# Silu in place on ScalarE, and the modulation pieces through ScalarE's DMA queue into three buffers

## What is computed

```
def swiglu(h, w_gate_up, w_down):
    gu = h @ w_gate_up
    gate, up = jnp.split(gu, 2, axis=-1)
    return (jax.nn.silu(gate) * up) @ w_down
```

```
mod = (jax.nn.silu(c.astype(F32)) @ ada_w.astype(F32) + ada_b.astype(F32)).astype(x.dtype)
```

## Time and profile before

| | |
|---|---|
| median of the timed runs | 1428.95 us |
| the profiled execution: own time, span | 1436.26 us, 1434.6 us |
| TensorE matmul busy | 1321.5 us (92%) |
| VectorE busy | 751.1 us (52%) |
| ScalarE busy | 510.2 us (36%) |
| GpSimd busy | 198.0 us (14%) |
| DMA | 364.40 MB, mean 254 GB/s |
| granted TensorE clock, mean | 0.968 of full speed |

### The profile page before, as it was taken

The page is one execution under the profiler, slowest core; times in us unless marked ns, Lnnn a source line. Parts: engine busy times, 40 slices in busy tenths (PEclk is TensorE's granted clock), DMA queues, the critical chain, the costliest instruction groups (busy, mean ns, idle before and its releaser), DMA issues.

```text
span 1434.6 us, 24642 instructions
## 1 busy us (share of the span) xinstructions
PE 1321.5 (92%) x10257; PEld 1017.1 (71%) x10260; DVE 751.1 (52%) x1297; ACT 510.2 (36%) x828; POOL 198.0 (14%) x96
## 2 busy tenths in 40 slices
PE   4989899799999799979998689999999999999997
PEld 3989899789899799878997579754444444444432
DVE  5767687657588768778994645511221212212113
ACT  2423333356543233347553542322222222222212
POOL 0000000000000000076866265100000000000002
PEclk7999999899999999989999999999999999999999
DMA  9776567243377806632422413619999999999994
GB/s 355 274 284 238 209 249 273 78 105 131 148 280 265 301 16 226 223 145 45 176 89 98 169 55 142 255 65 421 427 427 423 426 423 428 423 425 428 423 425 168
DMA packets 50640, 364.40 MB, mean 254 GB/s; under 512 B 7411, under 2 KB 8563, under 8 KB 23924
## 3 DMA queue, kind: packets, MB, share of 16 engines
q1 hardware_dynamic: 49828, 360.61, 63.3%
q0 software_dynamic: 720, 2.46, 0.9%
HBM read 360.35 MB, written 2.70 MB: 253 GB/s over the span
## 4 chain that ended last, share of the span: by engine, by line
PE 67%; DMA 12%; DVE 11%; issue 4%; ACT 3%; POOL 2%; SPq 0%; DVEq 0%; POOLq 0%
PE banks L1266 15%; DMA scr<-ada 9%; PE banks L724 9%; PE banks L726 8%; PE banks L725 8%; PE banks L1291 8%; PE banks L1217 4%; PE banks L1226 4%; DMA c_row<-small 2%; POOL slot_lo L636 2%; PE banks L702 1%; DVE scr L1764 1%; DVE slot_lo L1736 1%; PE banks L713 1%; PE banks L1232 1%
## 5 line engine op out<-in xcount | busy, mean ns | idle before, releaser
L726 PE MATMUL banks<-h_hi,slot_lo 128*128 128x256 f32 x704 | 200.3, 285 | 4.2 <-issue 4.2
L724 PE MATMUL banks<-h_hi,gu_hi 128*128 128x256 f32 x704 | 200.7, 285 | 3.2 <-issue 3.2
L725 PE MATMUL banks<-h_lo,gu_hi 128*128 128x256 f32 x704 | 200.2, 284 | 0.0
L2294 DVE TENSOR_TENSOR out_lo<-banks,out_hi 128x512 fp32r<-128x512 f32 x62 | 42.9, 692 | 185.2 <-ACT out_hi L1678 185.2
L726 PEld LDWEIGHTS banks<-h_hi,slot_lo 128*128 128x128 f32 x704 | 136.2, 193 | 4.5 <-issue 4.5
L724 PEld LDWEIGHTS banks<-h_hi,gu_hi 128*128 128x128 f32 x704 | 136.2, 193 | 4.0 <-issue 3.4
L726 PE MATMUL banks<-slot_lo,slot_lo 128*128 128x256 f32 x480 | 137.0, 285 | 0.0
L725 PEld LDWEIGHTS banks<-h_lo,gu_hi 128*128 128x128 f32 x704 | 136.2, 194 | 0.0
L724 PE MATMUL banks<-act_hi,down_hi 128*128 128x256 f32 x352 | 103.4, 294 | 20.6 <-DVE slot_lo L1736 20.6
L1291 PE MATMUL banks<-ring,scr 128*64 128x512 f32 x512 | 116.9, 598 | 1.9 <-ACT scr L1672 1.9
L1266 PE MATMUL banks<-ring,scr 128*64 128x512 f32 x512 | 112.6, 592 | 0.0
(11 more groups left out here) (418 smaller groups left out, 3001.1 us busy)
## 6 DMA issues: line engine op xcount, KB each, us to landing
ring<-experts SPq DMA_DIRECT2D x64, 2048.0 KB, 11.4
ring<-ws SPq DMA_DIRECT2D x77, 1536.0 KB, 7.1
ring<-experts SPq DMA_DIRECT2D x64, 1024.0 KB, 11.0
scr<-ada SPq DMA_DIRECT2D x96, 256.0 KB, 4.0
ring<-experts SPq DMA_DIRECT2D x1, 3072.0 KB, 9.9
scr<-bias_line POOLq DMA_DIRECT2D x4, 512.0 KB, 8.3
bias_line<-scr SPq DMA_DIRECT2D x1, 1536.0 KB
x<-xT SPq DMA_DIRECT2D x1, 1024.0 KB, 4.9
```

The lines of the kernel that those rows point to most:

```text
L724: nc.tensor.matmul(out, hi, move_hi, start=start, stop=False, skip_group_check=True)
L725: nc.tensor.matmul(out, hi, move_lo, start=False, stop=False, skip_group_check=True)
L726: return nc.tensor.matmul(out, lo, move_hi, start=False, stop=stop, skip_group_check=True)
L2294: ins = nc.vector.tensor_tensor(out_lo[part], B[6 + half], out_hi[part].bitcast(F32), ALU.subtract)
```

## The change

ScalarE makes `Silu` of the gate in place, so that VectorE's product L1781 and the tile `sig_f` in the network go. The 96 pieces and the four loads of `c_part` move from SyncE's queue to ScalarE's, with no wait of their own: ScalarE issues the pieces of step s+1 right behind the Silu of step s, ahead of the copy of the down weights. There are three buffers. VectorE takes all pieces of a step in one place, behind the split of gate and up: two or three in each of the steps 2 to 10. The sigmoid of `c` moves ahead of the first network, VectorE's product of it likewise, and `c_row` is written from ScalarE's queue behind `ffn_start`; ScalarE waits for it to land before it enters the network's loop. TensorE's part is unchanged.

```
-        c_part, ada_part = view(2304, ADA_COLS), [view(2816 + ADA_COLS * q, ADA_COLS) for q in range(2)]
+        c_part, ada_part = view(2304, ADA_COLS), [view(at, ADA_COLS) for at in (2816, 3328, 4352)]
...
+        ADA_STEPS = {s: range(8 * (s - 2) // 3, 8 * (s - 1) // 3) for s in range(2, RING)}
+        C_LOADS = 0
...
@@ SyncE: ada_before, ffn_2_ada and their calls go, and
-            sp.wait_ge(csil_ready, 1)
-            with nc.allow_non_contiguous_dma(reason="one column a chunk"):
-                sp.dma_start(c_row.rearrange("a (c p) -> p (a c)", p=P), csil).then_inc(csil_ready, 16)
-            sp.wait_ge(csil_ready, 17)
...
@@ ScalarE
                 if k in (1, 3, 6):
-                    load_table(ACT.Sigmoid)
+                    load_table(ACT.Silu if k < 6 else ACT.Sigmoid)
...
                         act.wait_ge(gr_ready, RING * i + (done + s + 1))
-                        nc.scalar.activation(sig_f[:, s % 2, :], gated[:, s % 2, :], ACT.Sigmoid).then_inc(sig_ready, 1)
+                        nc.scalar.activation(gated[:, s % 2, :], gated[:, s % 2, :], ACT.Silu).then_inc(sig_ready, 1)
+                        if s == 0:
+                            act.dma_start(c_part, c_row[0:1, bass.ds(ADA_COLS * i, ADA_COLS)].partition_broadcast(P)).then_inc(ada_landed[C_LOADS], 16)
+                        for p in ADA_STEPS.get(s + 1, ()):
+                            part = ada[ADA_PARTS * i + (2 * ADA_PARTS * (base // S_FFN2) + p)]
+                            act.dma_start(ada_part[p % 3], part).then_inc(ada_landed[p % 3], 16)
                         first_part(down_hi[s % 2], s, 2 * TILE, SLOT, down_hi_ready)
...
             norm_squares(0)
+            act.wait_ge(vec_loaded, 16)
+            nc.scalar.activation(csig, vecs[:, VEC["c"][0]:VEC["c"][1]], ACT.Sigmoid).then_inc(csil_ready, 1)
 
             act.wait_ge(pool_d, 4)
             ffn_start(S_FFN1)
+            act.wait_ge(csil_ready, 2)
+            with nc.allow_non_contiguous_dma(reason="one column a chunk"):
+                act.dma_start(c_row.rearrange("a (c p) -> p (a c)", p=P), csil).then_inc(csil_ready, 16)
             norm_squares(1, "norm_ffn0")
-            act.wait_ge(vec_loaded, 16)
-            nc.scalar.activation(csig, vecs[:, VEC["c"][0]:VEC["c"][1]], ACT.Sigmoid).then_inc(csig_ready, 1)
+            act.wait_ge(csil_ready, 18)
             ffn(S_FFN1, 0)
...
@@ VectorE
-                        modulation(s, 0, i)
+                        for p in ADA_STEPS.get(s, ()):
+                            modulation(p, i)
...
-                        step(1, nc.vector.tensor_tensor(gated[:, a, :], gated[:, a, :], sig_f[:, a, :], ALU.mult))
-                        step(2, nc.vector.tensor_tensor(act_raw, gated[:, a, :], up_r, ALU.mult))
-                        step(3, nc.vector.tensor_copy(act_hi[a], act_raw))
+                        dve.wait_ge(dve_step, 3 * RING * i + (steps[0] + 3 * s + 1))
+                        step(1, nc.vector.tensor_tensor(act_raw, gated[:, a, :], up_r, ALU.mult))
+                        step(2, nc.vector.tensor_copy(act_hi[a], act_raw))
                         nc.vector.tensor_tensor(act_lo[a], act_raw, act_hi[a].bitcast(F32), ALU.subtract).then_inc(act_ready, 1)
-                        modulation(s, 1, i)
                         dve.wait_ge(down_hi_ready, RING * i + (done + s + 1))
                         second_part(down_hi[a], s, 2 * TILE, SLOT, down_lo_ready)
-                        modulation(s, 2, i)
```

More of the change, by code:

```diff
@@ L356, in build @@
             sem(s) for s in ("s_ready", "s_used", "max_ready", "exp_ready", "p_ready", "pt_ready", "pts_ready", "o_ready", "o_copied"))
-        csig_ready, csil_ready, ada_used, mod_ready = (sem(s) for s in ("csig_ready", "csil_ready", "ada_weights_used", "mod_ready"))
-        ada_landed = [sem(f"ada_landed{q}") for q in range(2)]
+        csil_ready, ada_used, mod_ready = (sem(s) for s in ("csil_ready", "ada_weights_used", "mod_ready"))
+        ada_landed = [sem(f"ada_landed{q}") for q in range(3)]
         out_ready, out_done, rows_loaded, shared_done = (sem(s) for s in ("out_ready", "out_done", "rows_loaded", "shared_done"))
@@ L554, in _ @@
             load_after(S_FFN2 + 6, s_ready, HEADS_1 // 2)
-            def ffn_2_ada(units):
-                for unit in units:
-                    body, s = divmod(unit, RING)
-                    ada_before(s,
-                               lambda: sp.dma_start(c_part, c_row[0:1, body * ADA_COLS:(body + 1) * ADA_COLS].partition_broadcast(P)).then_inc(ada_landed[0], 16),
-                               lambda p: sp.dma_start(ada_part[p % 2], ada[ADA_PARTS * (2 + body) + p]).then_inc(ada_landed[p % 2], 16),
-                               lambda p: sp.wait_ge(ada_used, ADA_PARTS * (2 + body) + p + 2))
-            ada_units = 0
             for n in range(S_FFN2 + 7, N_SLOTS):
@@ L573, in _ @@
                         sp.dma_start(gate_row.rearrange("a (c p) -> p (a c)", p=P), mod[:, 40:48]).then_inc(rows_loaded, 16)
-                after = TENANT[n] + 1 if n >= S_FFN2 + RING else S_FFN2
-                if n < S_BR and after > S_FFN2 + ada_units:
-                    ffn_2_ada(range(ada_units, min(after - S_FFN2, FFN_CHUNKS)))
-                    ada_units = after - S_FFN2
-                load_after(n, w_used, after)
+                load_after(n, w_used, TENANT[n] + 1 if n >= S_FFN2 + RING else S_FFN2)
             def load_gate_up(u, e):
@@ L1774, in step @@
                             ins.then_inc(dve_step, 1)
-                            dve.wait_ge(dve_step, 4 * RING * i + (steps[0] + 4 * s + n + 1))
+                            dve.wait_ge(dve_step, 3 * RING * i + (steps[0] + 3 * s + n + 1))
                         dve.wait_ge(gu_ready, RING * i + (done + s + 1))
@@ L1887, in first_start @@
                 h_lo_pair(3)
-            def silu_of_c():
-                dve.wait_ge(csig_ready, 1)
-                nc.vector.tensor_tensor(csil, csig, vecs[:, VEC["c"][0]:VEC["c"][1]], ALU.mult).then_inc(csil_ready, 1)
-            ffn(S_FFN1, 0, 1, "norm_ffn0", first_start, silu_of_c, meanwhile=lambda: value_parts(0))
+            dve.wait_ge(csil_ready, 1)
+            nc.vector.tensor_tensor(csil, csig, vecs[:, VEC["c"][0]:VEC["c"][1]], ALU.mult).then_inc(csil_ready, 1)
+            ffn(S_FFN1, 0, 1, "norm_ffn0", first_start, meanwhile=lambda: value_parts(0))
             dve.wait_ge(rt_ready, 3)
```

19 lines of the change are left out of this document (8 added, 11 removed).

## The result

The changed kernel takes 1454.18 us (median of 4 runs, 1447.37 to 1457.57) against 1429.05 for the kernel before (4 runs, 1428.61 to 1429.69): a ratio of 1.017, interval 1.0131 to 1.0208. Forecast were 1427.9 us, in a range of 1403 to 1436. The change makes the kernel slower by 25 us, and the time is outside the range. The profiled run took 1455.65 us with a span of 1454.0, 19.4 more than the span before.

A forecast was written before the change was run, and what follows sets the result against it. Each feed-forward network was 190.1 us of TensorE work plus waits and lower clock, 215.2 and 205.3 us in all. First +1.4 (new c_row wait cancelling the gain), second -2.4: -1.0, giving 1427.9 us, range 1403 to 1436.

The forecast's parts named there:

- The wait for c_row: At the first network's loop entry: ScalarE waits for c_row, landing at 67, and TensorE stands 22.7 us.
- X: The time at which c_row lands, bounded by 45.8 and 70.2 us and taken as 67; TensorE's wait is X - 44.3.
- these 0.1 us a step cost nothing: Middle of a pass: VectorE's steps average 8.7 us with pieces against TensorE's 8.64, counted as 0.
- The allowance of 5.4 us: In a step, VectorE may be up to 5.4 us late before a down product waits.
- the ends: The four ends of passes: TensorE's waits fall to 0.7 each, one to 0.9, from 5.92, 4.21, 1.87 and 2.13.
- the bound of 15 us: Middle of a pass: if an issue costs twice as much, 36 steps lose some 15 us; 0 was taken.
- The pieces' latency: In each step: pieces land in 4.0 us median, wanted some 5.9 us behind the gate, so no wait.
- Rival E: First network's pass ends: pieces still land late and waits partly stay, some +4 us; chance 0.11 shared with another rival.
- rival C: Turn of the first network's passes: TensorE misses its own program, 11.2 us more, 1439 in all; chance 0.10.
- doesn't touch: Turn of the second network's passes: TensorE's list is unchanged, so the "issue" waits of 3.36 and 4.48 us count nothing.
- The clock: TensorE's lower clock: 2.4 us behind the c_row wait in the first network, 3.4 us in the second.
- rival A: Entry of the first network's loop: c_row lands early, up to 46; 24.6 us faster, 1404; chance 0.22.

The follow-up runs named there:

- e5: The changed kernel with the issues of c_part and the pieces behind ScalarE's copy of the down weights instead of ahead of it: 1434.65 us, ratio 1.0053 to before.
- e9: The changed kernel with issues behind the down copy, c_row issued early by SyncE and two ring loads held at the passes' turn: 1429.31 us, ratio 0.9983 to before.
- e11: The changed kernel with c_row written as 128 rows of 32 bytes and the issues behind ScalarE's down copy: 1421.61 us, ratio 0.9939 to before.
- e3: The changed kernel with c_part and the pieces issued by SyncE, one step earlier; ScalarE still waits for c_row: 1435.78 us, ratio 1.0036 to before.
- e0: The kernel before, unchanged, profiled once more: 1430.54 us.
- e4: e3 with c_row issued early by SyncE, ahead of nine ring loads, and no ScalarE wait for it: 1422.34 us, ratio 0.9948 to before.
- e8: e4 with the two ring loads at a pass's turn held until the next pass's first gate product, SyncE's loop written out: 1410.51 us, ratio 0.9874 to before.
- e10: e8 with the first c_part and first three pieces of the first network issued by ScalarE ahead of its loop: 1407.37 us, ratio 0.9844 to before.

## Why the prediction was wrong

**The wait for c_row: the mechanism held, the size was nearly right.** Forecast were a landing at 67 and 22.7 us of wait; measured are 63.2 and 19.14. 64 numbers an engine at 0.46 us each gave 63 in the forecast's own sum; the part of the tail that I added on top didn't come. That 63 was hit is partly luck: the issue came at 30.71, beside the split, and not behind it at 32.8, and the transfer took 32.5 us and not 29, 0.51 for each of 64. The Trainium skill (DMA: Bandwidth & Descriptors, "Queues, rings and completion order") would have had X near 46, with 9 to 17 descriptors to a turn. The trace doesn't agree: 32.5 us for 1024 numbers and 7.6 for 128 rows fit one descriptor to a turn much better, though no run counts the turns. Giving that rule a rival's chance and not the forecast was right, and the chance (0.22) was too high.

**"In the middle of a pass ... these 0.1 us a step cost nothing": this step failed.** Its sum had an error of its own: a step with two pieces has one piece and one issue less than one with three, 8.9 - 0.75 - 0.5 = 7.65, and I wrote 8.4. Rightly added up, the mean was 8.5 us a step, under TensorE's 8.64, and not 8.7. Measured are 9.28 over the seven steps from 84.81 to 149.79 (9.15 without their late piece), where the forecast's terms give 8.54. What was missing is the second wait: VectorE's own work and 1.2 us for three issues were counted, but not that ScalarE's gate and up copy ends 0.58 after VectorE's down split. Three issues took 1.65 on the mean of the first network (1.36 to 2.21), not 1.5. The allowance of 5.4 us by which VectorE may be late held, as long as a gate product follows: at 4.5 us of lag TensorE waits 0.46. But the last down product of a pass has none in front of it, and what is left of the lag is paid there. I took the ends at 0.7, and at 0.9 for one, from the order of VectorE's instructions alone. They were 4.43, 3.87, 4.42 and 4.55: 17.3 us where I had 3.0. The difference of 14.3 is near the bound of 15 us that I wrote and didn't take, and that is chance: the bound was for issues at twice the price, and its own terms, 36 x (1.5 - 0.9), give 21.6. That the order of the issues costs time is shown by e5: the same instructions in another order bring three ends to 0.83, and the time down by 1.2%.

**"The pieces' latency ... I take no wait" failed too.** VectorE waits 6.7 us for pieces in the first network, in six places, and 7.3 in the second; 8.0 of these 14.0 us stand ahead of the four ends. The median landing is 5.4 us, not 4.0, and in the last step, which has no gate and up split, a piece is wanted 4.4 us behind the gate (149.79 to 154.19), not 5.9. The chain that ended last goes through these transfers, the first end's among them:
```profile
150.39 5.78 DMA scr<-ada
```
In e5, e9 and e11 the ends that are left have late pieces too. Rival E had named it and priced it at 4. How the 14.3 us of the ends divide between this and the lag stays open, since e3 and e5 each mend both.

**The turn of the first network: rival C was half right.** I gave 0.10 to a wait for TensorE's program there. It came with 2.47 us, beside 1.24 for the low part of a split. That these waits are for the program is inferred: the profile marks them "issue", but it marks the ends of the passes so too, and those are waits for VectorE. That the change "doesn't touch" these waits was wrong: they are not an effect of one run (e0 has them), and they move with what the queues do at that moment (0 to 9.11 us over fourteen profiles). With two loads held back (and SyncE's loop written out) the two waits of e4's second network, 4.29 and 4.82, became 2.11 and 1.87 in e8, but 1.87 to 2.23 us of the longer one stayed in e8, e9 and e10, and e4's first network has none without it; whether the loads in flight are the cause or the phase isn't settled.

**The clock.** I counted 2.4 us behind one wait in the first network. 231.2 less 190.1 of work and 32.8 of waits leaves 8.3 for lower clock and short idle; in the second it is 7.4 where I had left 3.4. Each long wait brings its own stretch of it: in windows of 5 us the granted clock is 0.70 at 160, 0.73 at 170, 0.53 at 270 and 0.64 at 510.

Summed up for the first network: 216.6 forecast, less 3.6 (`c_row`), plus 6.9 (ends), 1.6 (three smaller waits of 0.41 to 0.77), 3.7 (turn) and 5.9 (clock): 231.1, with 231.2 measured. For the second: 202.9, plus 7.4 (ends), 0.3 (short waits), 4.0 (clock), less 5.4 (turn): 209.2, as measured. The shorter turn, which the forecast hadn't counted either, hides 5.4 us of what the second network lost.

**What held.** L1781 is gone, Silu costs what Sigmoid did, the extra table load at 32.56 costs nothing (the norm ends at 41 us in both), and nothing waits for a piece's buffer. The gain was there too: with both causes mended (e11) the kernel is 8.7 us faster than before by the ratio, and its two networks are 15 us shorter than in e0 in one profiled execution, where rival A had 24.6.

## What to carry to other kernels

Before issues are moved onto a compute engine, write out that engine's whole chain in one step, with every hand-over in both directions, and compare it with the step of the engine that sets the pace; then ask where a lag is paid, which is at the end of a loop and not in its middle. Look at the last step by itself: what it leaves out may have covered the landing of its data in the steps before. Put the issues behind the instruction that another engine waits for, not ahead of it. And an engine that splits weights must not wait in its own program for a transfer of single numbers that runs under a full stream.

## What the runs showed that I had not expected

- A write of 4 KB takes 32.5 us as 1024 single numbers and 7.6 us as 128 rows, beside the same loads; `gate_row`, 1024 numbers in a later stage, took 13.0.
- An issue on ScalarE runs beside the ACTIVATE in front of it: two issues (0.84 us) behind a copy of 1.05 hold the next one up by 0.18 us, while three ahead of a copy hold it up by 1.47 (1.98 at worst in the first network).
- A transfer issued at 42.89 behind nine loads on the same queue landed some 26 us later; the same pieces on ScalarE's queue landed after 17.6 us, and TensorE's wait of 5.90 became 0.60.
- At the end of a pass 0.83 us is the shortest wait, and it stands in seven of the kernels. I had worked out 0.7.
